# A transformer block on one core: an earlier split of the raw feed-forward weights, another order in the last quarter, and products of zeros at the start

## The reference

```python
h = concatenate([meta, x], axis=1)
hn = rmsnorm(h, mix_norm_g)
q, k, v, ca, cg = split(hn @ w_in)
attn = stick_breaking_attention(q, k, v)      # 8 heads of 64
conv = conformer_conv(ca, cg, ...)            # 512 channels, 31 taps
h = h + concatenate([attn, conv]) @ w_out
hn = rmsnorm(h, ffn_norm_g)
g = hn @ w_gate                               # 1024 x 2816
u = hn @ w_up
h = h + (silu(g) * u) @ w_down
out = rmsnorm(h, final_norm_g)[:, 16:]
```

## Time and profile before

| | us |
|---|---|
| median of 3 runs | 1189.51 (1189.15 to 1190.39) |
| the profiled execution, its own time | 1190.92 |
| its span in the trace | 1189.2 |
| TensorE busy (matmul) | 1159.6 |
| VectorE busy | 689.3 |
| GpSimd busy | 483.9 |
| ScalarE busy | 431.2 |

### The profile page before, as it was taken

How to read it: one execution, slowest core, us unless ns; L and a number is a source line. 1 busy time by engine, 2 the same in 40 slices (tenths; PEclk the granted TensorE clock), 3 DMA queues, 4 the chain that set the end, 5 groups by cost and what they waited for, 6 DMA issues and landing times.

```text
span 1189.2 us, 15351 instructions
## 1 busy us (share of the span) xinstructions
PE 1159.6 (98%) x5944; PEld 987.0 (83%) x5944; DVE 689.3 (58%) x744; ACT 431.2 (36%) x875; POOL 483.9 (41%) x370
## 2 busy tenths in 40 slices
PE   8999999999999999989999999999999999999997
PEld 6899899899898888768878787878787888888786
DVE  5339998998998656684343443434434343433347
ACT  6321553533737644453231313132222222221323
POOL 4116112202200023377364655556564647373822
PEclk9999999999999999999999999999999999999999
DMA  7203312203026011122111112121212121212114
GB/s 261 80 10 96 74 47 71 73 16 81 13 59 217 19 50 39 36 71 71 36 41 52 50 36 71 36 71 37 71 37 71 36 71 36 71 36 71 36 36 159
DMA packets 70911, 75.69 MB, mean 64 GB/s; under 512 B 11513, under 2 KB 60149, under 8 KB 70840
## 3 DMA queue, kind: packets, MB, share of 16 engines
q1 hardware_dynamic: 69656, 72.60, 19.7%
q10 hardware_dynamic: 1184, 2.13, 0.5%
HBM read 64.13 MB, written 6.32 MB: 59 GB/s over the span
## 4 chain that ended last, share of the span: by engine, by line
PE 69%; POOL 12%; DVE 10%; issue 8%; ACT 1%; DMA 0%; POOLq 0%; DVEq 0%; SPq 0%; ACTq 0%
PE ps L1829 20%; PE ps L1808 17%; PE ps L1613 15%; PE ps L1759 7%; DVE gq L1291 6%; PE ps L1570 4%; POOL wa_lo L645 4%; POOL wb_lo L645 2%; DVE acc L1212 2%; POOL wa_f L666 1%; POOL wa_f L660 1%; POOL wa_f L663 1%; PE ps L1692 1%; PE ps L1550 1%; PE ps L1660 1%
## 5 line engine op out<-in xcount | busy, mean ns | idle before, releaser
L1480 DVE TENSOR_TENSOR mix<-ps,mix 128x512 f32<-128x512 f32 x176 | 121.7, 691 | 138.5 <-PE ps L1829 138.5
L1212 DVE SCALAR_TENSOR_TENSOR acc<-u_pad,par,acc 128x1024 f32<-128x1024 f32 x116 | 152.8, 1360 | 1.5 <-ACT acc L836 1.4
L1829 PE MATMUL ps<-wd_hi,act_hi 128*128 128x512 f32 x352 | 137.0, 389 | 1.5 <-DVE act_lo L1469 1.5
L1829 PE MATMUL ps<-wd_hi,act_lo 128*128 128x512 f32 x352 | 136.9, 389 | 0.0
L1829 PE MATMUL ps<-wd_lo,act_hi 128*128 128x512 f32 x352 | 136.9, 389 | 0.0
L645 POOL TENSOR_TENSOR wa_lo<-wa_f,wa_hi 128x512 fp32r<-128x512 f32 x58 | 79.3, 1370 | 133.0 <-ACT wa_hi L1008 129.2
L587 POOL TENSOR_TENSOR wp_lo<-raw,wp_hi 128x1024 fp32r<-128x1024 f32 x16 | 48.9, 3057 | 194.3 <-ACT wp_hi L753 194.3
L1613 PE MATMUL ps<-hn_hi,wp_hi 128*128 128x348 f32 (+2 forms) x352 | 118.7, 337 | 0.0
L1613 PE MATMUL ps<-hn_lo,wp_hi 128*128 128x348 f32 (+2 forms) x352 | 117.7, 334 | 0.0
L1613 PE MATMUL ps<-hn_hi,wp_lo 128*128 128x348 f32 (+2 forms) x352 | 117.5, 334 | 0.0
L1291 DVE TENSOR_TENSOR_SCAN gq<-gq,ones 128x1040 f32<-128x1040 f32 (+4 forms) x64 | 98.1, 1562 | 4.5 <-ACT gq L917 4.4
(11 more groups left out here) (187 smaller groups left out, 2627.1 us busy)
## 6 DMA issues: line engine op xcount, KB each, us to landing
raw<-in_w_gate SPq DMA_DIRECT2D x11, 1024.0 KB, 5.3
raw<-in_w_up SPq DMA_DIRECT2D x11, 1024.0 KB, 5.3
wd_f<-in_w_down SPq DMA_DIRECT2D x11, 1024.0 KB, 4.9
raw<-in_w_in SPq DMA_DIRECT2D x16, 512.0 KB, 3.9
xin<-in_x SPq DMA_DIRECT2D x8, 512.0 KB, 10.0
wo_raw<-in_w_out SPq DMA_DIRECT2D x4, 1024.0 KB, 8.4
mix<-in_x SPq DMA_DIRECT2D x8, 512.0 KB, 3.7
out<-ost SPq DMA_DIRECT2D x7, 512.0 KB, 2.6
```

Of the source, the lines that this page charges most:

```text
L1212: dve.scalar_tensor_tensor(out=acc[:, j % 2, :], in0=u_pad[:, p % 2, j:j + L], scalar=par[:, p, j:j + 1], in1=acc[:, j % 2, :], op0=ALU.mu ...
L1480: dve.tensor_tensor(hrow, ps[:, TB + n % 4, :], hrow, ALU.add).then_inc(d_added, 1)
L1829: last = pe.matmul(ps[:, TB + n % 4, :], a[s][:, t, i * P:(i + 1) * P], w_[m][:, t, dh * BANK:(dh + 1) * BANK], start=(t == 0 and s == m = ...
```

## The change

Three edits.

1. From block 2 on, the high halves are made in the order 1, 5, 6, 2, 4, 7, 3 (before: 1, 5, 6, 2, 7, 3, 4), and GpSimd makes the low half of weight 4 right behind the last sum, ahead of the low halves of 7 and 3. TensorE's order stays.
2. In the last chunk only, VectorE makes the low half of quarter C12 before the product of quarter C21, and not behind it.
3. A tile of zeros, `idle`, is written by VectorE at the start, and TensorE multiplies it by itself into bank `PV`: three products before it waits for the constants, and seven behind the two that spread the gain row.

```diff
+        idle = keep("idle", [P, BANK], BF16)
...
         LATER = [(b, k) for b in range(2, BLOCKS) for k in IN_TURN]
+        LATER_W = [(b, k) for b in range(2, BLOCKS) for k in (1, 5, 6, 2, 4, 7, 3)]
...
-        PRODUCTS, HI_ORDER, LO_ORDER = FIRST_P + LATER, FIRST_HI + LATER, FIRST_LO + LATER
+        PRODUCTS, HI_ORDER, LO_ORDER = FIRST_P + LATER, FIRST_HI + LATER_W, FIRST_LO + LATER_W
...
                 weight_lo(b, 2)
                 weight_sum(b, 7)
+                weight_lo(b, 4)
                 weight_lo(b, 7)
                 weight_lo(b, 3)
-                weight_lo(b, 4)
...
         def _(dve):
+            dve.memset(idle[:, :], 0.0).then_inc(idle_ready, 1)
             dve.sem_inc(conv_step, 1)
...
-                    product(c, q)
-                    act_low(c, behind)
+                    if q == "C21" and c + 1 == CHUNKS:
+                        act_low(c, behind)
+                        product(c, q)
+                    else:
+                        product(c, q)
+                        act_low(c, behind)
                     behind = q
...
+            def keep_busy(n):
+                for _ in range(n):
+                    pe.matmul(ps[:, PV, :], idle[:, 0:P], idle[:, :], start=True, stop=True)
+
+            pe.wait_ge(idle_ready, 1)
+            keep_busy(3)
             pe.wait_ge(consts, 10)
             pe.wait_ge(g1_loaded, 16)
             for b in range(2):
                 pe.matmul(ps[:, PJ + b, :], ones_1[:, :], g1row[:, b * BANK:(b + 1) * BANK],
                           start=True, stop=True).then_inc(g1_spread, 1)
+            keep_busy(7)
```

More of the change, by code:

```diff
@@ L235, in hybrid_block @@
         wv_loaded, wvhi_done, wvlo_done = [sem(f"wv_loaded{j}") for j in range(4)], sem("wvhi_done"), sem("wvlo_done")
-        consts, par_t, par_ready = sem("consts"), sem("par_t"), sem("par_ready")
+        consts, idle_ready, par_t, par_ready = sem("consts"), sem("idle_ready"), sem("par_t"), sem("par_ready")
         x_sumsq, x_var, x_rstd, xn_ready = sem("x_sumsq"), sem("x_var"), sem("x_rstd"), sem("xn_ready")
```

## The result

| | before | changed |
|---|---|---|
| median, us | 1189.88 (1189.15 to 1190.39) | 1177.51 (1176.69 to 1177.89) |
| profiled execution: own time, span | 1190.92, 1189.2 | 1177.89, 1176.2 |
| block 3 to block 21, first product to first product | 551.23 | 539.74 |

The ratio of the medians is 0.9896, 95% interval 0.9879 to 0.9913: 12.4 us faster. The forecast was 1174.6, 14.9 faster (15.3 against the 1189.88 that this comparison gives the kernel before). The time lies in the range, just above what rival 1 gave (1176.1 to 1177.0).

A forecast was written before the change was run, and what follows sets the result against it. TensorE, busy 98% of the span, was taken to bound the kernel. Gains of 12.2 + 1.2 + 1.5 = 14.9 took the median from 1189.51 to a forecast 1174.6 us, range 1171.5 to 1181.0.

The forecast's parts named there:

- rival 1: Start: the clock doesn't come or doesn't stay, start worth 0 (to -0.9), 1176.1 to 1177.0; chance 0.23.
- What bounds the kernel: Whole kernel: TensorE's products fill 98% of the span; only its pauses and half-clock time can be won.
- Part 1: Nine gate blocks: late raw transfer delays products 5 and 6; new order issues it 3.96 us earlier, gaining 12.2.
- The cover for product 7: Up and gate blocks: low half 7, moved back, still ends 2.8 us before its product starts.
- rival 4: Blocks 2 to 21: product 7 starves because low 7 comes too late; slower, 1194.6 at 3.8 us late; chance 0.04.
- Rivals 2 and 3: Gate blocks: GpSimd stays late for product 6, 1180.3, chance 0.11; raw block isn't what holds the chain, 1186.8, chance 0.06.
- what is next late: Gate blocks after the earlier transfer: GpSimd has 4 us to spare for product 5, 1.9 for product 6.
- Part 2: Last quarter: swapping VectorE's low half of C12 ahead restarts TensorE earlier, gaining 1.2, bounds 1.0 and 1.7.
- Part 3: Start: products of zeros raise TensorE's clock before the first transposes at 8.77, gaining 1.5, at most 2.1.
- The bound of -0.9: Start: with the clock still low the seven zeros end at 9.4 to 9.6, 0.9 behind 8.77, without gain.
- the cap of 20.3: Start: VectorE's queue lets the products at 22.31 come at 20.3 at best, cutting TensorE's saving to 2.0.
- The range's lower end: Whole kernel: 1171.5, from all upper bounds (16.3, 1173.2) and 1.7 if the half-clock stretch of 513 doesn't recur.

The follow-up runs named there:

- the late transfer: Kernel before with the new order of halves on both engines, but the raw transfer held back to the last low half: 1189.87 us, ratio 0.9998.
- the high halves alone: Kernel before with the new order on ScalarE only, GpSimd keeping the old one: 1200.43 us against 1190.25, ratio 1.0083.
- edit 2: Kernel before with only the last chunk's swap on VectorE (low half of C12 before the product of C21): 1188.65 us, ratio 0.9989.
- edit 3: Kernel before with only the products of zeros at the start added: 1187.82 us, ratio 0.9982.
- both further edits: Changed kernel with five zeros behind the gain row and VectorE's C21 product ahead of C22's low half, except in the last chunk: 1176.29 us, ratio 0.9885.

## Why the prediction held, and where it was off

**What bounds the kernel:** right. By the products' lead, all the time won is TensorE's pauses and its first 20 us.

**Part 1, the cause:** right, and shown by the late transfer (gain gone) and by the high halves alone (transfer 1.25 later, 10.2 slower). The order of the halves by itself gave nothing: the late transfer's stretch is 0.9 shorter than before, and its transfers landed 0.9 sooner in sum. The issue was forecast at 779.0, 5.44 into the up block: 5.42. The cover for product 7 held; rival 4 did not come. Rivals 2 and 3 are out: product 6 is in time in all nine blocks, and the transfer was what held the chain.

**Part 1, the size:** 12.2 was forecast; 11.5 is the difference of the two profiles, and 10.9 that of the means (550.0 for the four profiles with the transfer at 9.40, 539.1 for the seven with edit 1 and the old order on VectorE). Two things were mis-sized. First, the profile of before and the three others lose 12.7, 11.7 (late transfer), 11.5 (edit 2) and 9.8 (edit 3) against 538.56, 11.4 on average; I took one of them for all. I had the median landing of 5.3 in the chain and did not ask how the nine differ, though product 5 passes each excess on. Second, "what is next late" lacked one line: I looked at GpSimd for product 5 (done 4 us early) and named the neighbours that stretch each other, but put the stretch only on GpSimd's side. On VectorE it makes the product of C21 late by 0.2 in up to four blocks, at most 1.2 in sum.

**Part 2:** right within 0.03 in the traces (1.17 for 1.2, with the restart's pause as forecast), 1.4 in its own measurement.

**Part 3 is the step that failed**, and in the traces it is rival 1. I wrote that eight microseconds of nearly unbroken products would lift the clock before 8.77. With three zeros in front they did so in none of seven profiles (with twenty behind it rose at 9.02). With three and seven zeros it rose at 9.28, 9.6, 10.13 and 15.47, with three and five at 11.12 and 15.76; without zeros at 16.2 to 18.1 (six profiles). The bound of -0.9 had the mechanism that I then left out of the value: the zeros end at 9.3 and hold the first tile back, to 9.30 or 9.31, in every profile with seven. The products of the second v tile, at 22.31 in the earlier trace rows, come at 21.0 to 21.9, mean 21.34, with seven zeros, and at 21.3 to 22.3, mean 21.87, without: 0.5 for the 1.5 that I took, a difference no larger than the spread within each group. The run times say more: 2.2 (1.2 to 3.2) for edit 3 alone, and 1.1, with overlapping intervals, beside the other edits. So the mechanism as I told it did not come, and what the zeros are worth is open between 0.5 and 2.2. That VectorE's queue caps the gain fits: in the profile where the clock rose soonest with seven zeros (9.28), TensorE has fast transposes from the first, and the products come at 20.97, near the cap of 20.3 plus the delay of 0.54.

As for the rule of the Trainium skill (TensorE: Matmul & The Clock Gate, Part 4: PE-mode transpose): the transposes of the first tile, with nothing but zeros and the gain row's products before them, ran at full speed in the profiles where the clock rose at 9.28 and 9.02, 16 in 1.63 in the latter, and the first real products behind them too. So it did not hold here: transposes with short pauses did not cost the clock. With 14 zeros in front it fell in the pause of 2.11 behind the one-row products. No run here shows transposes raising it.

**The sum** of the means is 10.9 + 1.2 + 0.5 = 12.6, for 12.4 and 13.4 measured. I had 14.9, and so the forecast of 1174.6 was 2.9 below the 1177.51 measured. It also took off the 1.4 by which the profiled execution was above the median; the slow landings of that execution, priced in the 12.2, are probably in part the same time, counted twice.

**The range's lower end** took in 1.7 us for the half-clock stretch near 513. Here it was worth nothing: see below.

## What to carry to other kernels

When an engine starves for data, follow the buffer back to its last reader. Here the order in which readers released a single buffer was worth more than the order in which their results were wanted, provided both engines of the split changed together (half of this edit cost 10 us). When a pause is priced from one profiled execution, look at each transfer's landing and not only at the median, and ask how much the figure moves in kernels where nothing of it was changed. Filling an engine to raise its clock has a price where the filling ends after the real work is ready: 0.5 us with seven zeros, 3.2 with twenty.

## What the runs showed of the hardware that I had not expected

**A half-clock stretch can be free.** The one of the earlier trace rows moved from kernel to kernel: it is at 513.1 before, 520.7 in the changed kernel, 613.6 with the high halves alone, and nowhere but at the very end in the kernel with both further edits. TensorE's rows of the changed kernel around its own (windows, and the product behind its pause):

```profile
519.54 0.47 PE L1824 MATMUL ps<-b_hi,wa_hi 128*128 128x512 f32 x1 [2.30 <-POOL wa_lo L648]
...
516.00:520.50 4.50, 2.20 (x10) 1.55 (x9) 4.50 (x4) 3.38 (x3) 2.85 (x2) 1.00 0.00 0
520.70:524.00 3.30, 3.30 (x9) 2.52 (x9) 3.30 (x3) 2.28 (x2) 2.00 (x2) 0.50 0.00 0
```

The lead over the kernel before, which has its own stretch first, goes from 0.38 to 1.90, 0.40, -1.21 and back to 0.37 within 18 us. VectorE is busy without a break from 505 to 525 and sets the pace: the product at 519.54 waits for GpSimd's low half, this for ScalarE's high half, and that stands in the queue behind one that waited 4.77 for VectorE's sums. What TensorE loses at half clock it waits less a moment later; the kernel before pauses 1.35 at 527.00, the changed one not at all. The kernel without such a stretch went into this part with a lead of 1.05 and came out of it, at 528.70, with the same 1.05.

**The clock can stay low under a busy TensorE.** With 14 zeros in front TensorE was busy for 3.63 of 4 and 4.00 of 4 us at 0.50 of the clock, from 12 to 20. No rule that I could read off the rows says when it comes back.
